# Eight first-chunk gate tiles in the last attention turn instead of four

## The reference

```python
h = rms_norm(x, g_pre[l], NORM_EPS)
proj = jnp.einsum('bsd,dn->bsn', h, w_in[l])
qa, ka, va, fa, za, qb, kb, vb, zb, gates = jnp.split(proj, SPLIT_POINTS, axis=-1)
...
ya = merge_heads(ya) * jax.nn.silu(za)
...
yb = merge_heads(yb) * jax.nn.silu(zb)
gate_a, gate_b = jnp.split(jax.nn.sigmoid(gates), N_BRANCHES, axis=-1)
merged = (gate_a * jnp.einsum('bsw,wd->bsd', ya, w_branch[l, 0])
          + gate_b * jnp.einsum('bsw,wd->bsd', yb, w_branch[l, 1]))
y = jnp.einsum('bsd,de->bse', merged, w_out[l])
x = x + rms_norm(y, g_post[l], NORM_EPS)
```

## Time and profile before

| what | us |
|---|---|
| median of 3 runs | 2488.58 (2487.76 to 2491.74) |
| span of the profiled execution | 2487.3 |
| last attention turn, 2034.97 to 2121.57 | 86.60 |
| merge chunk 0, 2121.57 to 2178.53 | 56.96 |
| merge chunk 1, 2178.53 to 2248.04 | 69.51 |
| merge chunk 2, 2248.04 to 2317.49 | 69.45 |
| TensorE busy over the span | 2326.8 (94%) |

### The profile page before, as it was taken

How to read it: one execution, slowest core, us unless ns; L and a number is a source line. 1 busy time by engine, 2 the same in 40 slices (tenths; PEclk the granted TensorE clock), 3 DMA queues, 4 the chain that set the end, 5 groups by cost and what they waited for, 6 DMA issues and landing times. The chain is left out here.

```text
span 2487.3 us, 33201 instructions
## 1 busy us (share of the span) xinstructions
PE 2326.8 (94%) x11754; PEld 1817.1 (73%) x11754; DVE 1022.1 (41%) x2882; ACT 825.4 (33%) x2128; POOL 242.1 (10%) x377
## 2 busy tenths in 40 slices
PE   7999999999979997999989799999999996899998
PEld 6877867768758886677767687767677664788877
DVE  4323224123233115455553326565656665333342
ACT  4121221221223013455542234544534443333232
POOL 1010010010010001121110000010000100011013
PEclk8999999999999998999999799999999999899999
DMA  3111211111135113011134401111011100443322
GB/s 138 37 51 51 66 42 49 55 46 53 46 116 210 68 60 127 9 50 50 48 115 131 160 21 38 58 42 41 24 42 59 42 8 8 145 119 111 100 90 90
DMA packets 125300, 175.12 MB, mean 70 GB/s; under 512 B 7576, under 2 KB 73176, under 8 KB 123616
## 3 DMA queue, kind: packets, MB, share of 16 engines
q1 hardware_dynamic: 119088, 157.39, 19.2%
q10 hardware_dynamic: 5200, 9.55, 1.0%
q0 software_dynamic: 864, 6.29, 0.7%
HBM read 143.79 MB, written 29.42 MB: 70 GB/s over the span
## 5 line engine op out<-in xcount | busy, mean ns | idle before, releaser
L91 PE MATMUL heads_p_ps<-ret_w_second_hi_sb,ret_hT_hi_sb 128*128 128x512 f32 x384 | 161.7, 421 | 0.2 <-DVE ret_w_second_lo_sb L477 0.2
L91 PE MATMUL heads_p_ps<-ret_w_second_lo_sb,ret_hT_hi_sb 128*128 128x512 f32 x384 | 149.9, 390 | 0.0
L91 PE MATMUL heads_p_ps<-ret_w_second_hi_sb,ret_hT_lo_sb 128*128 128x512 f32 x384 | 149.4, 389 | 0.0
L91 PE MATMUL att_proj_ps<-br_w_second_hi_sb,br_hT_hi_sb 128*128 128x512 f32 x256 | 110.5, 432 | 2.9 <-DVE br_w_second_lo_sb L2083 2.9
L2043 ACT ACTIVATE br_x_sb<-br_x_sb,att_max_neg_sb 128x256 f32<-128x256 f32 (+7 forms) x128 | 97.8, 768 | 21.3 <-DVE att_max_neg_sb L2256 21.3
L91 PE MATMUL att_proj_ps<-br_w_second_lo_sb,br_hT_hi_sb 128*128 128x512 f32 x256 | 100.6, 393 | 0.0
L91 PE MATMUL att_proj_ps<-br_w_second_hi_sb,br_hT_lo_sb 128*128 128x512 f32 x256 | 100.3, 392 | 0.0
L566 DVE SCALAR_TENSOR_TENSOR heads_state_sb<-heads_state_sb,heads_tab_sb,heads_kv_ps 128x512 f32<-128x512 f32 x48 | 33.7, 745 | 161.0 <-PE heads_o_ps L392 161.0
L2531 ACT ACTIVATE mrg_yT_hi_sb<-mrg_y_raw_sb 128x1024 fp32r<-128x1024 f32 x32 | 33.9, 1060 | 162.8 <-PE mrg_b_ps L2459 132.1
L91 PEld LDWEIGHTS heads_p_ps<-ret_w_second_hi_sb,ret_hT_hi_sb 128*128 128x128 f32 x384 | 72.1, 188 | 21.1 <-issue 7.3
L91 PEld LDWEIGHTS heads_p_ps<-ret_w_second_hi_sb,ret_hT_lo_sb 128*128 128x128 f32 x384 | 72.2, 188 | 20.9 <-issue 6.7
(11 more groups left out here) (447 smaller groups left out, 6313.9 us busy)
## 6 DMA issues: line engine op xcount, KB each, us to landing
early_w_kv_sb<-a_w_blocks SPq DMA_DIRECT2D x28, 1024.0 KB, 5.4
all_w_block_sb<-w_turns SPq DMA_DIRECT2D x12, 2048.0 KB, 9.6
mrg_y_raw_sb<-branch_yT_dram SPq DMA_DIRECT2D x32, 512.0 KB, 4.4
ret_o_dram<-early_x_rows_sb ACTq DMA_DIRECT2D x32, 256.0 KB, 2.4
all_w_block_sb<-swa_turns SPq DMA_DIRECT2D x4, 2048.0 KB, 9.7
ret_out_o_rows_sb<-ret_o_dram POOLq DMA_DIRECT2D x6, 1024.0 KB, 5.1
x_dram<-early_x_rows_sb SPq DMA_DIRECT2D x12, 512.0 KB, 3.0
heads_v_sb<-x SPq DMA_DIRECT2D x8, 512.0 KB, 4.2
```

The source lines that it names most:

```text
L91: mm = pe.matmul(out, rows[a], w[b], start=(k == 0 and a + b == 0), stop=(k == KT - 1 and b == 1))
```

## The change

The last turn projects a whole gate tile a step, 24 products in three parts (k 0 to 3, 4 to 6, 7), so all eight tiles of chunk 0; `first_gates` is gone. ScalarE copies each from the bank in the next step; tiles 4 to 7 go into the tensor `qkT_fox`, which no fox turn reads any more. At step 0 of the last turn SP also loads the gate weights of chunk 1, at step 2 the branch weights of chunk 0, at steps 4 and 5 the attention rows of tiles 0 and 1 for merge; the buffers of these loads are of their own now and not parts of x or of merge. At step 6 ScalarE and VectorE split k 0 to 3 of chunk 1's gate weights, and the other four in t = 0 and 1 of chunk 0. In chunk 0 of merge TensorE runs only branch products and transposes. SP loads the weights of chunk 2 without waiting for the last splits of a chunk ago. To make room, `log_f` lies in `zT`, and the descriptor memory of GpSimd's transfers is made smaller; `o_rows` of the first layer is loaded by ScalarE's queue behind its copies instead of GpSimd's.

```diff
@@ -652,11 +652,6 @@
         @block.gpsimd
         def _(pool):
-            for t in range(2, TILES):
-
-                pool.wait_ge(oT_tr, 4 * (t - 1) if t == 2 else 4 * t)
-                pool.dma_start(o_rows[:], o_dram[t * P:(t + 1) * P, :]).then_inc(o_in, 16)
-                pool.wait_ge(o_in, 16 * (t - 1))
             pool.memset(minus_half[:], -0.5).then_inc(half_set, 1)
             pool.wait_ge(half_set, 1)
...
@@ -727,7 +722,12 @@
                     act.wait_ge(oT_tr, 4 * t + n + 1)
                     act.activation(oT[t % 2][0][:, 4 * n:4 * n + 4, :], p_tr[n][:].rearrange("p (k n) -> p k n", k=4), ACT.Copy).then_inc(oT_hi, 1)
+            def load_next(t):
+
+                act.dma_start(o_rows[:], o_dram[t * P:(t + 1) * P, :]).then_inc(o_in, 16)
+
             copy_rows(0)
+            load_next(2)
             copy_rows(1)
             for n in range(len(splits)):
                 if n in (0, 2 * KT):
...
@@ -745,6 +745,8 @@
             for t in range(2, TILES):
                 copy_rows(t)
+                if t + 1 < TILES:
+                    load_next(t + 1)
...
+        y_raw = mem.sb("y_raw", P, 2, 2 * PAIRS, P)
+        w_br_raw = mem.sb("w_br_raw", P, 2 * PAIRS, MERGE_COLS)
+        ahead_in = [nc.alloc_semaphore(name=f"br_{name}") for name in ("y_in0", "y_in1", "wbr_in")]
+
+
+        gates_0 = [half.rearrange("p t n -> p (t n)").rearrange("p (t n) -> p t n", n=BANK) for half in (x[:, 4:6, :], qkT_fox[:])]
         def w_at(fox, k):
             return [part[:, k % (KT // 2), :] for part in (w_first[fox] if k < KT // 2 else w_second)]
-        attend(nc, x, ident, dram, hT, w_raw, w_at, stats[1], gates_0, yT_dram)
-        merge(nc, x, ident, dram, hT, w_raw, w_at, w_first, gates_0, yT_dram, y_post)
...
@@ -1721,10 +1734,17 @@
                         row = done.number(1, 0 if done.fox else PAIRS)
                         sp.dma_start(yT_dram[bass.ds(row, 1), :, u * P:(u + 1) * P].rearrange("a p n -> (a p) n"),
                                      yT[:, u % 2, :]).then_inc(y_out[u % 2], 16)
-                    if t == 0 and following:
-
-                        sp.wait_ge(w_lo, following.order(KT, KT))
-                        load_w(following.next())
+                    if t == 0:
+
+                        filling = following or GATES
+                        sp.wait_ge(w_lo, filling.order(KT, KT))
+                        load_w(filling.next())
+                    if not following and t == 2:
+                        sp.dma_start(w_br_raw[:], merge_blocks(dram)[:, :, 0, :]).then_inc(ahead_in[2], 16)
+                    if not following and t in (4, 5):
+
+                        sp.wait_ge(y_out[t % 2], turn.order(16 * TILES // 2, 16))
+                        sp.dma_start(y_raw[:, t % 2], yT_dram.rearrange("k p n -> p k n")[:, :, (t - 4) * P:(t - 3) * P]).then_inc(ahead_in[t % 2], 16)
...
@@ -1905,26 +1920,22 @@
                         scores(t)
                     if last:
                         transpose_probs(*last, 0)
-                    if following:
-                        project(following, t, range(0, 4))
-                    elif t < TILES:
-                        first_gates(t, 0)
+                    if t < TILES:
+                        project(following or GATES, t, range(0, 4))
...
                         transpose_probs(*last, 4)
-                    if following:
-                        project(following, t, range(4, 7))
-                    elif t < TILES:
-                        first_gates(t, 1)
+                    if t < TILES:
+                        project(following or GATES, t, range(4, 7))
                     if last:
                         values(*last)
                     if t < TILES and projected(turn, following, t):
                         transpose_qk(*projected(turn, following, t))
-                    if following:
-                        project(following, t, range(7, KT))
+                    if t < TILES:
+                        project(following or GATES, t, range(7, KT))
...
                 act.wait_ge(proj_done, GATES.tiles(t + 1))
                 if t == 0:
                     act.wait_ge(logits_done, GATES.tiles(-TILES))
-                act.activation(gates_0[:, t, :], p_proj[:], ACT.Copy).then_inc(vz_done, 1)
+                if t == TILES // 2:
+                    act.wait_ge(s_done, GATES.tiles(-TILES))
+                act.activation(gates_0[t // 4][:, t % 4, :], p_proj[:], ACT.Copy).then_inc(vz_done, 1)
...
                     done = t < TILES and projected(turn, following, t)
                     if done:
                         copy_projection(*done)
-                    if not following and t in range(2, 2 * GATES_AHEAD + 1, 2):
-                        copy_gates(t // 2 - 1)
+                    if not following and 1 <= t <= TILES:
+                        copy_gates(t - 1)
...
                     if last and not last[0].fox:
                         mean_square(*last)
-                    if t == TILES - 2 and following:
-                        split_high(following.next(), range(0, 4))
+                    if t == TILES - 2:
+                        split_high((following or GATES).next(), range(0, 4))
...
@@ -2296,32 +2309,30 @@
...
-                    if t == TILES - 2 and following:
-                        split_low(following.next(), range(0, 4))
+                    if t == TILES - 2:
+                        split_low((following or GATES).next(), range(0, 4))
...
@@ -2379,19 +2390,15 @@
             def chunk_sync(c):
                 for t in range(TILES):
-                    load_rows(c, t)
-                    if t == 0:
-                        if c.is_at(0):
-                            load_branches(c)
+                    if not c.is_at(0) or t >= RAWS:
+                        load_rows(c, t)
+                    if t == 0 and not c.is_at(0):
+                        sp.wait_ge(w_lo, c.times(KT, -KT // 2))
+                        if c.is_at(CHUNKS - 1):
+                            sp.dma_start(w_raw[:], w_out[:, :, 0:BANK]).then_inc(wo_in, 16)
                         else:
-                            sp.wait_ge(w_lo, c.times(KT))
-                            if c.is_at(CHUNKS - 1):
-                                sp.dma_start(w_raw[:], w_out[:, :, 0:BANK]).then_inc(wo_in, 16)
-                            else:
-                                load_gates(c.plus(1))
+                            load_gates(c.plus(1))
                     if t == 3:
-                        if c.is_at(0):
-                            load_gates(c.plus(1))
                         if not c.is_at(CHUNKS - 1):
                             sp.wait_ge(wbr_lo, c.times(2, 2))
                             load_branches(c.plus(1))
...
@@ -2461,22 +2468,19 @@
                 mm.then_inc(br_done, 1)
             def gates(c, t):
-                if not c.is_at(0) or t >= GATES_AHEAD + 2:
+                if not c.is_at(1) or t >= 2:
                     at_least(pe, sig_done, c.times(TILES, t - 1))
                 for k in range(KT):
-                    if t == 0 and not c.is_at(0):
-
-                        pe.wait_ge(w_lo, c.times(KT, k + 1 - KT))
+                    if t == 0:
+
+                        at_least(pe, w_lo, c.times(KT, k + 1 - KT - KT // 2))
                     mm = products(pe, p_gate[t % 2][:], at_tile(hT, slice(t * P, (t + 1) * P)), lambda k: gate_w(c, k), (k,))
                 mm.then_inc(gate_done, 1)
             def chunk_pe(c):
                 for t in range(TILES):
-                    if not c.is_at(0) or t >= GATES_AHEAD + 2:
+                    if not c.is_at(0):
                         gates(c, t)
-                    elif t in (0, 3):
-
-                        gates(c, GATES_AHEAD + t // 3)
                     if t == 0 and not c.is_at(0):
                         transpose_merged(c.plus(-1), TILES - 1)
...
@@ -2550,17 +2554,19 @@
                     if not (c.is_at(CHUNKS - 1) and t == TILES - 1):
                         split_rows(c, t + 1)
                     at_least(act, merged_done, c.times(TILES, t - 1))
-                    if c.is_at(0) and t < GATES_AHEAD:
-                        logits = gates_0[:, t, :]
+                    if c.is_at(0):
+                        logits = gates_0[t // 4][:, t % 4, :]
                     else:
-                        act.wait_ge(gate_done, c.times(TILES, t + 1 - GATES_AHEAD))
+                        act.wait_ge(gate_done, c.times(TILES, t + 1 - TILES))
                         logits = p_gate[t % 2][:]
                     act.activation(sig[:, t % 2, :], logits, ACT.Sigmoid).then_inc(sig_done, 1)
                     if t >= 2:
                         copy_merged(c, t - 2)
-                    if t in (3, 4) and not c.is_at(CHUNKS - 1):
+                    if t in (3, 4) and not c.is_at(CHUNKS - 1) and not c.is_at(0):
                         split_gates(c.plus(1), range(2 * (t - 3), 2 * (t - 2)))
```

(6 more changed lines are left out.)

42 lines of the change are left out of this document (21 added, 21 removed).

## The result

The changed kernel takes **2473.98 us** in the median (2472.37 to 2475.21, 4 runs) against 2488.17 (2485.69 to 2491.74, 4 runs) before: ratio 0.9942, 95% interval 0.9929 to 0.9955. The change saves 14.2 us; 17.0 on 2488.58 had been forecast. The profiled execution after has a span of 2470.6 us against 2487.3 before, 16.7 less. Each run's time lies 1.8 above its own span (2472.37 against 2470.6).

The account below looks back on a forecast made before the run. Chunk 1 was taken as TensorE-bound, the last turn as bound by VectorE's loop, with TensorE waiting. -23.2 + 3.7 + 2.5 = -17.0 on a span of 2487.3 gave 2470.3, median 2471.6 us, range 2466 to 2481.

Parts of the forecast that it names:

- Chunk 0: Merge chunk 0 without its four gate tiles and with earlier loads: 33.8 us against 56.96, -23.2, bounds -28.2 and -9.0.
- Start 4.8: Chunk 0, from its barrier to the first branch product: 4.8 us, with 4.4 of landing gone.
- Branches 0 and 1: Chunk 0: branch 0 at 1.2 GHz takes 5.1 us, branch 1 at full clock 3.0.
- Branch 2 with its pause: Chunk 0: 0.7 pause behind VectorE's product and low halves, plus 3.0 of work, 3.7 us.
- Branches 4 to 7: Chunk 0: loading y rows through two buffers binds over TensorE's 3.0, 3.4 us each, 13.6 in all.
- The clock rival: Chunk 0: pauses bring the clock down in every branch, chunk 0 takes 48.0, total 2485.8 us; chance 0.10.
- The turn: Last attention turn: four more gate tiles, 24 products a step instead of 12, cost +3.7 us, bounds 0 and 5.7.
- The split at step 6: Last turn: four low halves of chunk 1's gate weights stand in VectorE's loop, +2.5 us, bounds 0 and 2.5.
- Part 4: The rest: SP's loads in the turn, first layer's output rows on ScalarE's queue, log_f's tile, smaller descriptor memory: 0.
- signs of being wrong: Turn grows by more than 9, chunk 0 stays above 40, or another stage moves by more than 1.
- The slower rival: Last turn becomes TensorE-bound at 1.2 GHz, eight steps about +36, total 2507 us; chance 0.04.
- Change not doing what it says: Chunk 0's first y rows still wait behind SP's stores; 4.4 comes back, 2476 us, inside the range.

Follow-up runs that it names:

- e6: Changed kernel, but chunk 0 has four buffers for its y rows, with rows 2 and 3 loaded at the barrier; 2472.15 us (2 runs).
- e1: Changed kernel, but the first half of chunk 1's gate weights is split in step 8 of the last turn, not step 6; 2470.89 us, ratio 0.9924.
- e2: Kernel before, with only the first layer's output rows 2 to 7 loaded from ScalarE's queue and the smaller descriptor memory; 2491.25 us, ratio 1.0011.
- e4: Changed kernel, but in the last turn three products of gate tiles 0 and 1 follow the next scores, and values(0) moves ahead in step 1; 2474.95 us.
- e8: e4's order, plus in step 2 the transpose of att_y(0) ahead of gate tile 2 and values(1) ahead of its second part; 2474.94 us (2 runs).
- e9: Changed kernel, but gate tile 0 spread over steps 0 and 1, tiles 1 to 6 in steps 2 to 7, tile 7 in step 8; 2472.04 us, ratio 0.9932.
- e5: Changed kernel, but ScalarE issues the first layer's output row 2 load behind all high halves of that layer's weights; 2471.64 us, ratio 0.9930.
- e11: Kernel before with e2's queue change, but row 2 issued behind ScalarE's first copy of row 1; 2488.20 us (8 runs), ratio 0.9997.

## Why the prediction held, and where it did not

**Chunk 0 (-23.2; measured -24.2 with the entrance).** Built up as 33.8, it took 32.79; the same code took 32.6 to 34.2 in five more traces, so the 1.0 is within the scatter. Start 4.8: measured 4.64. Branches 0 and 1, 5.1 + 3.0: 48 products in 7.25; the clock rose inside branch 0, not behind it. Branch 2 with its pause 3.7: 4.0. Branch 3, 3.5: 3.48. Branches 4 to 7 at 3.4 by the load loop, 13.6: 13.4, and e6 showed that this loop binds and that TensorE alone would give 3.09 a tile. It was right to take the landing of the rows from the trace: 4.2 us in the median, 4.4 in the earlier trace rows, where the formula of the Trainium skill (DMA: Bandwidth & Descriptors, Anatomy of one DMA) gives 3.2. There the Trainium skill states it for transfers that GpSimd issues; these rows are SyncE's, which the prediction does not say.

**The clock rival (2485.8).** Chunk 0 had pauses of 0.2 to 0.64 between branches, 1.39 in e1, and the clock stayed at 1.00. What the Trainium skill (TensorE: Matmul & The Clock Gate, A second HAM failure mode: psum-queue depth-cycling) reports of another kernel, small idle spells that keep the clock falling and rising, did not happen there. In e2 the clock was down behind one pause of 4.46.

**The turn (+3.7; measured +3.4 in steps 0 to 3, -0.3 in the tail).** Logits(1) +1.47 against 1.2, step 1 +1.59 against 1.8, steps 2 and 3 +0.27 and +0.03 against 0.45 and 0.25. The sizes were right and the reading behind them too narrow. The prediction told it as positions in queues, which another order would cure; e4 and e8 showed that two other orders don't, and e9 that fewer products in steps 0 and 1 do. The fill per step was worked out in the prediction, but only for steps 2 to 4 and not for the two that grew.

**The split at step 6 (+2.5).** The step grew by 2.40; e1 took 2.39 of it back.

**Part 4 (0, with 1 either way) is the step that failed.** "The output rows of the first layer move from GpSimd's queue to ScalarE's ... 0" rested on the time between trigger and use of the rows, 10.9 us. That held: nobody waited for row 2. What was not asked is who is behind it at the DMA engines: the 2 MB of weights that TensorE's third group waits for. "The first of them falls into the weight loads there" named the place and gave it no price. The price is 1.8 to 3.7 in eight of nine traces, enough to account for the 2.4 us by which the median, 2473.98, misses 2471.6. e5, the changed kernel with that load moved, came to 2471.64; its interval overlaps the changed kernel's, so the medians alone don't prove it. The expectation for e2, 1.0 to 1.8, was still too low: the delay alone was 2.1, and the clock added 1.6. One of the prediction's own signs of being wrong, another stage moving by more than 1, came true here.

**The sum.** That the profiled span met the forecast (2470.6 against 2470.3) is luck. The turn came out 0.7 below its term, chunk 0 1.0 and the chunks behind it 0.5 (chunk 1 took 68.64, not 69.5); the first layer came out 1.8 above and the rest 0.7. It was also the fastest run, with a cheap passage of the first layer (39.12, where most took 40 to 41). And the 1.3 that turned the span into a median was in part scatter: as a run's time lies 1.8 above its own span, the profiled execution of the kernel before stands for 2489.1, not for the median.

**The slower rival** (2507, TensorE at 1.2 GHz in the turn) did not come: the clock is at 1.00 from 2034 to 2102. **Change not doing what it says**: the y rows were there at the barrier.

## What to carry to other kernels

Filler for idle time has to be measured out by the idle time of each step: equal portions of 24 products overfilled the two steps that had only about 1 us idle, while the tail, with TensorE busy 12.98 of 20.42 us, had room left. A load that nobody waits for need not be free where the DMA engines are full; look at what is behind it, not at what depends on it. And when reorderings give back what they gain, look whether the engine is full; here it was, and moving work out of the stretch helped.

## What the runs showed of the hardware

- DMA at its limit: with some 390 GB/s moving, 1 MB issued on another queue 7.8 us behind a load of 2 MB put that load off by 2.1 us (13.4 to 15.5 from issue to use, e2); in eight traces with ScalarE's issue 7.6 to 9.0 us behind it was 15.2 to 16.7. Issued 10.0 us behind it, it did not (13.3, e11). That the 2 MB were issued earlier did not protect them.
- TensorE's clock after a pause, in the first layer's third group over all fourteen traces: 24 products behind a pause of 0.68 to 2.94 us took 5.57 to 5.62, behind one of 4.32 to 4.53 they took 7.16 to 7.20. This holds for that place: in merge chunk 0 of the kernel before, the branch product behind a pause of only 1.74 ran at 0.62 of the clock.
- The clock and the entrance: with the same work behind the barrier, branches 0 and 1 took between 7.14 (e5) and 8.01 us (e6). In the attention turns before, single groups of twelve gate or projection products ran at the lower level in one execution and not in the next, each worth 1.5 us (one such group took 4.35 from 1628.72 in the kernel before and 2.86 from 1629.50 in the changed one); a difference of that size in one profile says nothing.
